# Gathering two experts' rows at once, and a weight ring in strict order: a mixture-of-experts decoder on one core

## The reference

```
logits = xt @ w_router;  top_vals, top_idx = top_k(logits, 2);  gates = softmax(top_vals)
combine = sum(one_hot(top_idx, 8) * gates[..., None], axis=1)
for e in range(8):
    gu = xt @ w_gu[e]                       # 1024 -> 2 * 2816
    y = y + combine[:, e:e+1] * ((silu(g) * u) @ w_down[e])
h = h + y
h = h + sigmoid(rmsnorm(h, norm_ple) @ w_ple_gate) * (p @ w_ple_up)
```

## Time and profile before

| what | value |
|---|---|
| median of 3 runs | 1171.66 us (1171.53 to 1172.48) |
| the profiled execution's own time | 1171.78 us |
| its span, first to last instruction | 1169.7 us |
| PE busy / PEld / DVE / ACT | 96% / 53% / 26% / 19% |
| chain of work that ended last | PE 91%, DVE 3%, DMA 2% |
| weights by DMA | 342.22 MB, mean 294 GB/s |
| the experts, from the first gather to the last scatter | 451 to 1135 us |

### The profile page before, as it was taken

One profiled execution on the slowest core, in us unless ns is written; L12 is line 12 of the kernel. 1 busy time (PEld: TensorE's weight loads), 2 busy tenths in 40 slices (PEclk: granted clock), 3 DMA queues, 4 the chain that ended last, 5 costly groups with the idle time before them and its releaser, 6 DMA issues.

```text
span 1169.7 us, 21411 instructions
## 1 busy us (share of the span) xinstructions
PE 1119.3 (96%) x9605; PEld 617.1 (53%) x9606; DVE 299.0 (26%) x527; ACT 224.3 (19%) x350; POOL 9.4 (1%) x53
## 2 busy tenths in 40 slices
PE   7887999999999899999999999999999999999968
PEld 5556999998588455343334343353344343353426
DVE  4664544453323524000100100100100100100143
ACT  2352444443222612000000000000000000000033
POOL 3000000000000000000000000000000000000000
PEclk9978999999999999999999999999999999999999
DMA  9805556654142308599999999999999999999950
GB/s 332 291 1 180 181 182 192 201 179 147 36 181 73 144 1 323 191 405 420 417 418 407 410 418 419 417 418 420 414 400 328 417 419 419 417 419 419 417 241 36
DMA packets 114025, 343.63 MB, mean 294 GB/s; under 512 B 7757, under 2 KB 30858, under 8 KB 113930
## 3 DMA queue, kind: packets, MB, share of 16 engines
q1 hardware_dynamic: 113930, 342.22, 74.7%
HBM read 341.15 MB, written 1.05 MB: 293 GB/s over the span
## 4 chain that ended last, share of the span: by engine, by line
PE 91%; DVE 3%; DMA 2%; ACT 1%; SPq 1%; issue 1%; DVEq 0%; ACTq 0%
PE ps L1813 34%; PE ps L1864 12%; PE ps L1563 6%; PE ps L1564 6%; PE ps L1565 6%; PE ps L1547 6%; PE ps L1869 4%; PE ps L1794 3%; PE ps L1683 2%; DMA wring<-in_w_exp_down 2%; PE ps L1837 1%; SPq L378 1%; PE ps L1882 1%; PE ps L1438 1%; PE ps L1460 1%
## 5 line engine op out<-in xcount | busy, mean ns | idle before, releaser
L1813 PE MATMUL ps<-wring,xg 128*32 128x512 f32 (+1 forms) x4704 | 416.3, 502 | 1.5 <-DVE e_h L1286 1.5
L1813 PEld LDWEIGHTS ps<-wring,xg 128*32 128x32 f32 x4704 | 155.6, 110 | 242.2 <-issue 198.1
L1864 PE MATMUL ps<-wring,ehT 128*32 128x512 f32 x1408 | 164.6, 594 | 4.8 <-DMA wring<-in_w_exp_down 4.2
L1563 PE MATMUL ps<-dn_high,w_high 128*128 128x256 f32 x352 | 100.7, 286 | 2.5 <-DVE dn_low L1106 2.5
L1564 PE MATMUL ps<-dn_low,w_high 128*128 128x256 f32 x352 | 100.5, 286 | 0.0
L1565 PE MATMUL ps<-dn_high,w_low 128*128 128x256 f32 x352 | 100.4, 285 | 0.0
L1864 PEld LDWEIGHTS ps<-wring,ehT 128*32 128x32 f32 x1408 | 43.7, 110 | 103.9 <-issue 92.7
L1097 DVE TENSOR_TENSOR w_low<-ring,w_high 128x2048 fp32r<-128x2048 f32 x33 | 75.5, 2292 | 58.3 <-ACT w_high L685 58.3
L802 ACT COPY ehT<-ps 128x384 f32<-128x384 f32 (+1 forms) x24 | 10.5, 439 | 379.3 <-PE ps L1837 266.0
L1298 DVE COPY ehT<-ps 128x384 f32<-128x384 f32 (+3 forms) x24 | 10.8, 450 | 261.9 <-PE ps L1837 192.7
L1563 PEld LDWEIGHTS ps<-dn_high,w_high 128*128 128x128 f32 x352 | 68.5, 195 | 3.3 <-DVE dn_low L1106 2.9
(11 more groups left out here) (288 smaller groups left out, 961.0 us busy)
## 6 DMA issues: line engine op xcount, KB each, us to landing
wring<-in_w_exp_gu SPq DMA_DIRECT2D x128, 1024.0 KB, 16.6
wring<-in_w_exp_down SPq DMA_DIRECT2D x88, 1024.0 KB, 15.6
wring<-in_w_exp_gu SPq DMA_DIRECT2D x64, 768.0 KB, 14.1
ring<-in_w_ffn_gu SPq DMA_DIRECT2D x44, 512.0 KB, 5.0
ring<-in_w_ffn_down SPq DMA_DIRECT2D x11, 1024.0 KB, 4.9
ring<-in_w_ple_gate SPq DMA_DIRECT2D x4, 1024.0 KB, 4.8
ring<-in_w_q_b SPq DMA_DIRECT2D x4, 1024.0 KB, 5.1
ring<-in_w_o_b SPq DMA_DIRECT2D x4, 1024.0 KB, 6.1
```

The source lines that it names most:

```text
L1563: pe.matmul(out, high_l, high_r, start=first, stop=False)
L1813: return pe.matmul(ps[32 * quarter:32 * quarter + 32, bank, c0:c0 + 2 * nf * P], xg[:, k, 32 * b:32 * b + 32], w[:, :, f * P:(f + nf) * P] ...
L1864: ins = pe.matmul(ps[32 * q:32 * q + 32, 3, :], turned(g, 2 * u + r, b, nb), w[:, r, half * 512:(half + 1) * 512], start=(g == 0 and u == ...
```

## The change

Five things change together.

- **The ring.** The first seven units loaded early are those of group 1 (from the second on); the eight of group 0 and the first of group 1 follow after the attention's output product. Places are set so that the first expert's units are freed in the same order as those of all others, and the list "first" is gone. The waits of the experts behind it are the same numbers as before.
- **The gather.** `hs` becomes `hs_high` (fp32r, by ScalarE) and `hs_low` (the rest, by VectorE, `rows_low`). `pick` is fp32r and holds two experts, `xg` too. Experts 1 and 2, 3 and 4, 5 and 6 of the order (`PAIRS`) are gathered by one `gather_pair` in four quarters of two chunks, one in front of each unit of down 1: 192 columns, high and low part, two token tiles. Experts 0 and 7 are gathered alone, now with high and low parts.
- **The first gather** waits for ScalarE's copy of the embedding only in its second half.
- **The end.** The transposes and the gate product (`gate_tail`) stand in a block of their own for the case without further passes, directly behind the last scatter; the jump over the loop comes behind them.
- **Memory.** `hs_high` and `hs_low` lie over `hs` and `hnT`; `lower` and `gains_raw` move into the region that the ring takes over.

```
-    place = {("lead", "gu", 0, k): (2048 * (k + 1)) % (8 * 2048) for k in range(KD)}
-    place.update({("lead", "gu", 1, k): 1024 * 17 + 2048 * k for k in range(KD)})
+    place = {("lead", "gu", 0, k): 1024 * 17 + 2048 * k for k in range(KD)}
+    place.update({("lead", "gu", 1, k): 2048 * k for k in range(KD)})
...
-    gu2_first = (13, 13, 14, 15, 16, 16, 8, 8)
-    free["first"] = [9, 10, 11, 12, *gu2_first, 2, 3, 4, 5, 6, 7, *range(17, 23), 24, 25, 26, *range(28, 36)]
     free["body"] = [1, 2, 3, 4, 5, 5, 6, 7, 8, 8, 9, 10, *range(11, 15), *range(15, 23), 24, 25, 26, *range(28, 36)]
...
-        for k, (name, g, u) in enumerate(LEAD):
-            if k < 7:
-                sp_.wait_ge(*released(*order[45 + k]))
-            elif k == 7:
-                sp_.wait_ge(o_b_ready, NT)
-            expert_dma(sp_, "lead", name, g, u, FIRST)
+        for k in range(1, KD):
+            sp_.wait_ge(*released(*order[44 + k]))
+            expert_dma(sp_, "lead", "gu", 1, k, FIRST)
+        sp_.wait_ge(o_b_ready, NT)
+        for k in range(KD):
+            expert_dma(sp_, "lead", "gu", 0, k, FIRST)
+        expert_dma(sp_, "lead", "gu", 1, 0, FIRST)
...
+        def rows_low(t):
+            dve.wait_ge(hs_done, 4 * NT + t + 1)
+            dve.wait_ge(lg_ready, NT)
+            dve.scalar_tensor_tensor(out=hs_low[:, t, :], in0=h[:, t, :], scalar=rstd[:, 4, t:t + 1], in1=hs_high[:, t, :].bitcast(F32),
+                                     op0=ALU.mult, op1=ALU.subtract).then_inc(hn_low_done, 1)
...
+        def gather_pair(k, r):
+            pe.wait_ge(e_pick, k + 2)
+            if r:
+                pe.wait_ge(e_xg_done, k * 2 + r)
+            else:
+                pe.wait_ge(e_pickT_done, k)
+            for c in range(2):
+                cols = slice((2 * r + c) * P, (2 * r + c + 1) * P)
+                o = ps[:, 7, c * 2 * SLOTS:(c + 1) * 2 * SLOTS].rearrange("p (e n) -> p e n", e=2)
+                for i, rows_ in enumerate((hs_high, hs_low)):
+                    for t in range(NT):
+                        ins = pe.matmul(o, rows_[:, t, cols], pick[:, t, :, 64:64 + SLOTS], start=(i == 0 and t == 0), stop=(i == 1 and t == NT - 1))
+            ins.then_inc(e_xg, 1)
...
-            gather(n + 1, 0, nb2)
-            down("body", 1, n, nb, range(0, 2))
-            gather(n + 1, 1, nb2)
-            down("body", 1, n, nb, range(2, 4))
+            for u in range(4):
+                if n + 1 in PAIRS:
+                    gather_pair(n + 1, u)
+                elif n + 1 == E - 1 and u % 2 == 0:
+                    gather(n + 1, u // 2, nb2)
+                down("body", 1, n, nb, range(u, u + 1))
...
+        with pe.If(largest == 0):
+            gate_tail(E, 1)
         with pe.If(largest > 0):
```

More of the change, by code:

```diff
@@ L485, in _ @@
             after = sp_.value_load(expert_at[0:1, n + 1:n + 2], min_val=0, max_val=E - 1)
-            loads("body", BODY, n, lambda i: after if BODY[i][0] == "gu" and BODY[i][1] < 2 else e, "body" if n else "first")
+            loads("body", BODY, n, lambda i: after if BODY[i][0] == "gu" and BODY[i][1] < 2 else e, "body")
             e = after
@@ L1334, in both_experts @@
             product(2, n, nb)
-            for half in range(2):
-                gathered(n + 1, half, nb2)
+            if n + 1 in PAIRS:
+                gathered_pair(n + 1)
+            elif n + 1 == E - 1:
+                for half in range(2):
+                    gathered(n + 1, half, nb2)
             turned_high(2, n, nb)
@@ L1943, in _, with gate_tail @@
         last_groups(E - 1, TILES[E - 1], "end")
-        preps = pe.alloc_register("preps_pe")
-        pe.reg_mov(preps, 1)
-        passes = pe.alloc_register("passes_pe")
-        pe.reg_mov(passes, E)
+        def gate_tail(n, ready):
+            for t in range(NT):
+                pe.wait_ge(e_added, n * 2 - (1 - t))
+                for half in range(2):
+                    for c in range(4):
+                        k = 4 * half + c
+                        ins = pe.transpose(ps[:, 3 + 2 * t + half, c * P:(c + 1) * P], h[:, t, k * P:(k + 1) * P], ident[:])
+                    ins.then_inc(x_turned, 1)
+            pe.wait_ge(t_low, ready * KD)
+            for t in range(NT):
+                pe.wait_ge(x_low_done, 2 * t + 2)
+                tok = slice(t * P, (t + 1) * P)
+                for half in range(2):
+                    cols = slice(half * 512, (half + 1) * 512)
+                    for k in range(KD):
+                        ins = passes3(ps[:, 3 + 2 * t + half, :], x_high[:, k, tok], x_low[:, k, tok], gate_high[:, k, cols], gate_low[:, k, cols],
+                                      k == 0, k == KD - 1)
+                    ins.then_inc(gate_ready, 1)
+        with pe.If(largest == 0):
+            gate_tail(E, 1)
         with pe.If(largest > 0):
+            passes = pe.alloc_register("passes_pe")
+            pe.reg_mov(passes, E)
             with pe.Fori(0, E) as i:
@@ L1956, in _ @@
                         pe.reg_add(passes, passes, 1)
[L1957 to L1976 removed]
+            gate_tail(pe.snap(passes), 2)
     es.close()
```

100 lines of the change are left out of this document (53 added, 47 removed).

## The result

The changed kernel takes 1161.2 us in the median of four runs (1160.59 to 1162.61), the kernel before 1171.6 (1171.03 to 1172.48): ratio 0.9912, 95% interval 0.9895 to 0.9929. Measured once more beside the experiments, on five runs, it took 1161.5 against 1170.7: ratio 0.9922, 0.9908 to 0.9936. The profiled execution has a span of 1158.5 us where before had 1169.7.

The account below looks back on a forecast made before the run. The DMA stream was taken to set the end, tied to TensorE's pace at the full ring near 886 us. Gathers 7.5 + start 0.5 + end 2.5 = 10.5 us off 1171.7 gives 1161.2 us; range 1155 to 1173.

Parts of the forecast that it names:

- the full ring: Near 886 us the weight stream lacks room, so TensorE's pace there sets the end; closing the earlier 20 us hole gains nothing.
- the start: At the first expert's gather: waiting for the second low part instead of ScalarE's copy gains 0.5 us (0 to 0.9).
- the end: After the last scatter: without the jump, transposes and gate product start earlier, 2.5 us gained (between 0.2 and 3.9).
- The losses: The stream, 20 us ahead, fills the ring sooner and stands there, near 510 to 560 us.
- the ring gives its 20 us: Rival: the stream is no longer bound by room and TensorE alone sets the end, 18.6 us gained, 1153.1 us; chance 0.03.
- The gathers: Experts 1 to 6 gathered in pairs at 3.96 us each; net 7.5 us gained up to the full ring.
- The price of the matmul: In the paired gather's quarters, an fp32r matmul of 192 columns was taken at 0.120 us, between 0.090 and 0.328.
- f32's price: Rival in the twelve quarters: a narrow fp32r matmul costs 0.328 us as f32 does, 1182.5 us; chance 0.20.
- half of it: Rival in the twelve quarters: 0.164 us a matmul, 3.3 us gained instead of 7.5, 1165.4 us; chance 0.08.
- VectorE's own skip: At the end VectorE must pass its own much shorter skipped block before its pieces; it was there by 1141.31 at the latest.
- The larger gain of 3.9: At the end: if VectorE's short skip costs little, the gain is nearer 3.9 us, the sum 1.4 us lower.
- The low clock at the last units: Rival: after a 5.7 us wait the last seven units run at 1.2 GHz; all slow loses 7.4 us, 1168.6; chance 0.08.

Follow-up runs that it names:

- The ring alone: Kernel before with only the new order, places and shares of the weight ring: 1171.53 us against 1170.82, ratio 1.0008.
- the unpaired kernel: Changed kernel with every expert gathered by itself, still in fp32r high and low parts: 1167.43 us, ratio 0.9966.
- the f32 pairs: Changed kernel with experts still gathered two at once, but from f32 rows and picks without low parts: 1165.7 us, ratio 0.995.
- the last version above: Changed kernel with expert sizes reordered to tiles (3,2,3,3,2,3,3,2) and the first expert alone gathered from f32 rows: 1150.77 us, ratio 0.9828.

## Why the prediction was right, point by point

The time was 1161.2, as predicted, and the mechanism of the full ring held in every test. The terms did not all hold: two were too large, the start even with the wrong sign, and the end, between the two profiled executions, was too small.

- **The full ring.** Right. The ring alone gives nothing, the same 3.6 us cost 4 us in front of 890 us and nothing that can be told behind it, and when the sizes are reordered so that the stream does not run short there, the end moves by the 9 us worked out for it. The wait ahead of the last seven units came as written (5.7 predicted, 6.07). The losses came as well, but over more time than the 510 to 560 us written: from 490 to 650 us they are 19.7 us, summed as for the ring alone. The last full ring stands at 870 to 900, not 870 to 890. The rival that the ring gives its 20 us fell.
- **The gathers: 7.5 predicted, 6.3 measured.** The price of the matmul was right (0.120 taken, 0.1125 measured), and with it the rivals of f32's price and of half of it fell. Mis-sized was the piece: I measured a piece from its start to the next unit's start, which leaves out what the change of work costs ahead of it. In the trace of before a unit with half a gather takes 4.65 us (532.32 to 536.97), 2.07 more than the 2.58 of a plain one and not 1.95 more; a quarter costs 1.20 and not 0.99. The part of a piece's own time that does not grow with its matmuls was taken too small as well: 1.06 is 8 x 0.1125 + 0.16, and the prediction had 8 x 0.12 + 0.03. Four pieces instead of two have twice these fixed parts: a pair is 4.8 us and not 3.96, a single gather 4.14 (two tiles: 4.06) and not 3.9; 3 x 4.14 + 2 x 4.06 - 3 x 4.8 = 6.1, near the 6.3 measured.
- **The start: 0.5 predicted, 0.8 lost.** The first unit starts 1.92 us earlier, of which 1.56 are the front's scatter, so 0.36 is gained. Then the clock, which no step of the prediction spoke of at this place, takes 1.2 us back: 22.01 instead of 20.81 us for the 192 matmuls.
- **The end: 2.5 predicted; 3.9 between the two profiled executions, 2.3 in the test that undoes it, 3.4 by its times.** The step was right and its size is open by about a microsecond and a half, because the idle time at the jump itself varies (2.60, 2.93, 4.15 us). What the prediction held back for VectorE's own skip was not lost: its x_low starts 0.17 us behind the sums (1130.43, the sums from 1127.78 for 2.48), and the product 1.61 us behind them, where the prediction's best case had 1.65 (its 1137.5 + 2 x 0.7 is 1138.9 and not 1139.1). The larger gain of 3.9 is met by one pair of traces and not by the other. The Trainium skill (Runtime: NRT & Kernel Launch, Instruction fetch mechanics) has the rule that went with it: a taken branch to a target outside the pages held must fetch the page first. The traces agree: in all three with the jump the profile has a packet on its instruction queue q8 (0.02 MB) within 1 us behind the start of the last scatter's matmul, and in the changed kernel none there; that TensorE waits for this packet is not shown. The jump that now stands behind the gate product shows no cost: from that product's start to the span's end it is 26.63 us after and 26.70 before.
- **The low clock at the last units.** The mechanism came, the loss did not, as the prediction had it for a few slow units: 0.50 is granted at 1108 to 1112 us behind the wait of 6.07, and the seven units still start 2.48 us apart.

So 6.3 - 0.8 + 2.3 to 3.9 is 7.8 to 9.4 us, where the two measurements say 10.4 and 9.2. The agreement of the first median with the forecast to the tenth is luck: an excess of 1.2 in the gathers and 1.3 in the start were met by the end and by scatter.

## What to carry to other kernels

Where a stream of transfers runs ahead through a ring, find the last place at which the ring is full. As long as the consumer still waits for the stream behind that place, here work added or taken away before it moved the end, and a hole in the stream before it or work behind it did not. The cheapest gain may be an order of the work in which the consumer never falls so far behind at one place. Price a small piece of work by the difference between a stretch with it and one without, never from its start to the next start. Before an instruction type is made cheaper, see which of its sides bounds it: here an fp32r matmul took 0.1125 us at 64, 96 and 192 columns alike, which I take for the price of its weight load (the weight loads are busy for 2.00 of 2.00 us in the gather's window, 450 to 452), so that only more columns per load help.

## What the hardware showed that was not expected

TensorE's clock fell to 0.50 while the engine was busy but for 0.17 us. In the changed kernel it fell at the end of the gather of 448 to 452.8 us, 32 fp32r matmuls of 96 columns with one wait of 0.17 us for VectorE in it: 0.96 was granted at 450 to 452 and 0.50 at 452 to 454; in the unpaired kernel the same gather was followed by 0.50 at 454 to 458 and 23.5 us instead of 20.8 for the first units. The same number of records in f32 with the same columns kept 1.00, in every kernel that had them there (before, the ring alone, the f32 pairs, the last version above). The Trainium skill (TensorE: Matmul & The Clock Gate, Part 1: The HAM clock gate) says that the clock is halved when the engine has been idle. By the profile's busy column it was hardly idle here (1.83 of 2.00 us at 448 to 450, 2.00 in each window from 450 on), so a full busy column does not promise the full clock. The wait alone is not the cause: in the kernel before TensorE idled 0.88 us just ahead of its f32 gather and kept 1.00. But no run has the fp32r gather without its wait, so that the form of the matmuls is the cause is likely and not shown.

The clock also differs at the end: without the jump the sixteen transposes take 2.28 us in the changed kernel and 3.5 us in the last version above, 0.50 granted in the latter, with almost the same wait ahead of them (0.92 and 0.91 us). What decides this was not tested.
